# One block on one core: TensorE adds the rows of an expert pair before it runs the second tile's stage of that pair, and VectorE and ScalarE take its results one pair later

## What is computed

```
q = (ht @ w_q).reshape(T, PEER_HEADS, 2, PEER_HALF)
sc = jnp.einsum('thpc,hpnc->thpn', q, sub_keys)
s1, i1 = lax.top_k(sc[:, :, 0], 16);  s2, i2 = lax.top_k(sc[:, :, 1], 16)
top_s, pos = lax.top_k(s1[..., :, None] + s2[..., None, :], 16)   # flattened
eid = take_along_axis(i1 * 128 + i2, pos);  g = softmax(top_s)
a = einsum('cd,chkd->chk', hc, u_tab[ec])
y = einsum('chk,chkd->cd', gc * gelu(a), v_tab[ec])
x = x + gate2 * y
```

## Time and profile before

| | |
|---|---|
| median of three runs | 1017.3 us (1014.5 to 1018.57) |
| the profiled execution | 1019.0 us, span of its instructions 1017.2 us |
| busy: TensorE matmul / VectorE / ScalarE / GpSimd | 841.0 / 649.5 / 362.3 / 288.1 us |
| DMA | 351.95 MB, mean 346 GB/s |
| gathers of expert rows | 268.45 MB |

### The profile page before, as it was taken

The page is one execution under the profiler, slowest core; times in us unless marked ns, Lnnn a source line. Parts: engine busy times, 40 slices in busy tenths (PEclk is TensorE's granted clock), DMA queues, the critical chain, the costliest instruction groups (busy, mean ns, idle before and its releaser), DMA issues.

```text
span 1017.2 us, 9145 instructions
## 1 busy us (share of the span) xinstructions
PE 841.0 (83%) x2764; PEld 470.4 (46%) x2764; DVE 649.5 (64%) x1612; ACT 362.3 (36%) x1015; POOL 288.1 (28%) x275
## 2 busy tenths in 40 slices
PE   4889889998978888878987975988698777777776
PEld 4767656657943333333434533653263332222222
DVE  4799957723868587777543643975778644455444
ACT  2456434532235545654221231341233222222221
POOL 3000000000223334424422531335245343333330
PEclk9999979998998899979998987999899899999999
DMA  9958845547779699978999997999989999999995
GB/s 318 384 204 311 313 168 191 207 152 265 273 309 421 253 373 377 420 283 342 419 411 400 400 410 265 379 418 409 422 338 423 392 423 422 422 420 422 421 422 238
DMA packets 84872, 351.95 MB, mean 346 GB/s; under 512 B 6668, under 2 KB 19028, under 8 KB 52056
## 3 DMA queue, kind: packets, MB, share of 16 engines
q0 software_dynamic: 36864, 268.45, 65.2%
q1 hardware_dynamic: 46264, 82.89, 23.1%
q10 hardware_dynamic: 1696, 0.04, 0.1%
HBM read 350.31 MB, written 1.05 MB: 345 GB/s over the span
## 4 chain that ended last, share of the span: by engine, by line
PE 43%; DMA 27%; DVE 21%; issue 4%; ACT 3%; POOL 1%; ACTq 1%; SPq 1%; POOLq 0%; DVEq 0%
PE ps_y L1415 18%; DMA ring<-in_peer_uv,eid 15%; DVE ring L869 6%; DMA late_ring<-in_w_peer_q 4%; DMA out_y<-wide 3%; DMA late_ring<-in_w_out 3%; PE bank L1355 3%; PE bank L1364 2%; DMA late_ring<-in_w_up_moba 2%; PE bank L1380 2%; PE ps_y L1226 2%; PE bank L1226 2%; PE ps_y L1227 2%; PE ps_y L1228 2%; PE bank L1227 2%
## 5 line engine op out<-in xcount | busy, mean ns | idle before, releaser
L1415 PE MATMUL ps_y<-ring,diag 128*128 128x512 f32 x1024 | 491.4, 629 | 114.2 <-ACT diag L1130 112.9
L493 POOL DMA_INDIRECT ring<-in_peer_uv,eid x256 | 278.5, 1088 | 690.0 <-PE ps_y L1415 416.8
L869 DVE CUSTOM_DVE_ANT_0 ring<-ring,gates 128x1024 f32<-128x1024 f32 x256 | 307.7, 1224 | 183.8 <-DMA ring<-in_peer_uv,eid 182.7
L1415 PEld LDWEIGHTS ps_y<-ring,diag 128*128 128x128 f32 x1024 | 197.2, 200 | 382.9 <-issue 211.5
L1119 ACT ACTIVATE gel<-adot 128x2 f32<-128x2 f32 x128 | 26.0, 203 | 394.3 <-DVE adot L869 394.1
L1130 ACT ACTIVATE diag<-ident,ew 128x128 f32<-128x128 f32 x256 | 86.7, 386 | 0.0
L1123 ACT ACTIVATE ew<-g_sb,gel 128x1 f32<-128x1 f32 x256 | 61.5, 287 | 4.2
L956 ACT ACTIVATE w_hi<-ring 128x512 fp32r<-128x512 f32 x80 | 47.9, 626 | 29.5 <-PE bank L1228 28.1
L554 DVE TENSOR_TENSOR w_lo<-ring,w_hi 128x512 fp32r<-128x512 f32 x80 | 54.4, 690 | 4.4 <-PE ps_y L1228 1.9
L1226 PE MATMUL bank<-w_hi,hT_hi 128*128 128x512 f32 x96 | 40.4, 421 | 7.0 <-DVE w_lo L554 4.0
L1380 PE MATMUL bank<-tT,late_ring 128*128 128x128 f32 x256 | 31.6, 284 | 12.7 <-DMA late_ring<-in_w_peer_q 12.7
(11 more groups left out here) (184 smaller groups left out, 859.8 us busy)
## 6 DMA issues: line engine op xcount, KB each, us to landing
ring<-in_w_ada SPq DMA_DIRECT2D x12, 2048.0 KB, 9.0
ring<-in_w_in SPq DMA_DIRECT2D x10, 2048.0 KB, 8.0
ring<-in_w_peer_q SPq DMA_DIRECT2D x4, 2048.0 KB, 8.1
late_ring<-in_w_peer_q SPq DMA_DIRECT2D x8, 1024.0 KB, 21.8
ring<-in_w_out SPq DMA_DIRECT2D x2, 2048.0 KB, 10.8
ring<-in_peer_uv,eid POOLq DMA_INDIRECT x256
late_ring<-in_w_out SPq DMA_DIRECT2D x4, 1024.0 KB, 17.5
ring<-in_w_up_fox SPq DMA_DIRECT2D x1, 2048.0 KB, 9.1
```

Of the source, the lines that this page charges most:

```text
L493: pool.indirect_dma_start(uv_row(n), None, peer_uv, bass.IndirectOffsetOnAxis(ap=eid[:, n:n + 1], axis=0)).then_inc(s_uv[n % NP], 16)
L869: dve.tensor_tensor_reduce(u_row(n), u_row(n), h2[:, n // P, :], 1.0, 0.0, ALU.mult, ALU.add, adot[:, at:at + 1]).then_inc(s_dot, 1)
L1415: ins = pe.matmul(ps_y[:, cut], diag[:, n % ND, :], v_row(n)[:, cut], start=first, stop=last)
```

## The change

TensorE's loop now calls `add_rows(pair)` first and the stages of that slot after it. VectorE's and ScalarE's stages that take TensorE's results are laid one slot later, so that each is as far behind TensorE's as it was. `norm2`, tile 1's first choices (heads 0 and 1) and the first `choose_keys` of the loop move one slot later too. The other choices keep their slots: tile 0's at 4, 6, 13, 15, 17, 24, 26, 28, tile 1's at 59 to 82. So does `finish(0)` at 64. No instruction is added or removed.

```
-    "up": (35, 36, 39, 40), "up_dve": (36, 37, 40, 41),
+    "up": (35, 36, 39, 40), "up_dve": (37, 38, 41, 42),
     "mix": (40, 42),
-    "out": (43, 44, 47, 48), "out_dve": (44, 45, 48, 49),
-    "norm2": 50, "h2T": 51,
+    "out": (43, 44, 47, 48), "out_dve": (45, 46, 49, 50),
+    "norm2": 51, "h2T": 51,
     "queries1": (52, 53, 56, 57, 62, 63, 74, 75),
-    "keys": ((None, None, 2, 13, 24), (54, 59, 69, 78)),
-    "pairs": ((None, None, 4, 15, 26), (55, 61, 71, 80)),
-    "experts": ((None, None, 6, 17, 28), (56, 62, 73, 82)),
+    "keys": ((None, None, 3, 13, 24), (55, 59, 69, 78)),
+    "pairs": ((None, None, 4, 15, 26), (56, 61, 71, 80)),
+    "experts": ((None, None, 6, 17, 28), (57, 62, 73, 82)),
...
-def lay_attention(behind, attention):
+def lay_attention(behind, attention, later=0):
     for n, slot in enumerate(SLOT["attention"]):
-        lay(behind, slot, lambda n=n: attention(1, n // STEPS, range(n % STEPS, n % STEPS + 1)))
+        lay(behind, slot + later, lambda n=n: attention(1, n // STEPS, range(n % STEPS, n % STEPS + 1)))
...
-            lay_attention(behind, attention)
+            lay_attention(behind, attention, 1)
...
-                lay(behind, SLOT["queries0"][m - Q_FIRST], lambda m=m: queries(0, m))
-            lay_attention(behind, attention)
+                lay(behind, SLOT["queries0"][m - Q_FIRST] + 1, lambda m=m: queries(0, m))
+            lay_attention(behind, attention, 1)
             for h in range(2):
-                lay(behind, SLOT["mix"][h], lambda h=h: to_tT(1, "mixT", h))
-                lay(behind, SLOT["h2T"], lambda h=h: to_tT(1, "h2T", h))
+                lay(behind, SLOT["mix"][h] + 1, lambda h=h: to_tT(1, "mixT", h))
+                lay(behind, SLOT["h2T"] + 1, lambda h=h: to_tT(1, "h2T", h))
             lay(behind, SLOT["norm2"], norm2_root)
             for m in range(8):
-                lay(behind, SLOT["queries1"][m], lambda m=m: queries(1, m))
+                lay(behind, SLOT["queries1"][m] + 1, lambda m=m: queries(1, m))
...
             for pair in range(NG * PAIRS):
-                for stage in behind.get(pair, ()):
-                    stage()
                 if pair == HEADS * PAIRS:
                     pe.wait_ge(s_ytaken, 2)
                 add_rows(pair)
+                for stage in behind.get(pair, ()):
+                    stage()
```

## The result

| | median | lowest to highest | ratio to before, 95% interval |
|---|---|---|---|
| before, same chip | 1015.9 us (4 runs) | 1008.1 to 1018.6 | |
| changed kernel | 1035.1 us (4 runs) | 1031.2 to 1040.6 | 1.0206 [1.0132, 1.0280] |
| changed kernel, timed again | 1037.1 us (6 runs) | 1032.8 to 1037.7 | 1.0214 [1.0184, 1.0243] |

The changed kernel is 2.1% slower, 19 to 22 us by the medians. The forecast was 14 us, 1031.3, in a range of 1019 to 1041.

What follows compares the result with a forecast made beforehand. Gathers were taken to fill the DMA for most of the second half, so cost was priced as DMA idle time. Start 8.5, tile 0's choices 2, store 1.5, pairs 74 and 75 2: 1017.3 + 14 = 1031.3 us, range 1019 to 1041.

Steps and rivals of the forecast that it cites:

- The start: First pairs: tile 0's last queries run after adds, row 6 is issued later, first adds slow; 8.5 us, from 6 to 10.
- row 22: Tile 0's early gathers: row 22, issued at 338.65 before, comes some 7.4 us later, near 346.
- three waits: VectorE at score tiles: step 16's 5.70 us falls to some 2; steps 11 and 18 each get about 5.
- Tile 0's choices: Choices keeping their slots: net 6 us more waiting on VectorE, more than half hidden; 2 us, from -6 to +6.
- Pairs 63 to 75: Tile 1's later queries, late load and store: 1.5 us idle DMA for the store, 2 us at pairs 74 and 75.
- pair 63: Query moved from before pair 63's adds to before pair 64's, about 3 us later; costed at nothing, 3 if uncovered.
- pairs 74 and 75: Query now after pair 74's adds, adds of 76 to 78 3.7 us later; 2 us idle DMA, 0 to 4.
- The store term: VectorE at slot 71 waits 6 to 12 us for tile 0's stores, before 3.93; 1.5 us idle DMA, 0 to 5.
- (a): Rival, whole kernel: only the start costs, the moved choices cancel; 1021 to 1025 us, chance 0.16.
- (b): Rival, slot 26: separating step 16 from choose_pairs closes idle time, if row 6 comes before 297; 1013 us, chance 0.07.
- (c): Rival: slot 71 store wait uncovered (8), slot 59 keys stall 3, tile 0's waits in full (6); 1047 us, chance 0.09.
- (d): Rival, whole kernel: gathers fill the DMA whatever TensorE's order, so no change; 1017 us, chance 0.06.

Runs made afterwards that it cites:

- e12: Changed kernel with the start repaired, query blocks 4 to 7 of tile 1 one slot earlier; 1019.3 us, ratio 1.0034.
- e1: Kernel before with only the last two query blocks of tile 0 one pair later; 1023.4 us, ratio 1.0069.
- e3: Changed kernel with all later choices of VectorE one slot later too, start left late; 1023.2 us, ratio 1.0070.
- e4: Changed kernel with tile 0's last two query blocks back at the start and all choices one slot later; 1014.6 us, ratio 0.9991.
- e2: Changed kernel with the last two query blocks of tile 0 back ahead of the adds of pairs 0 and 1; 1023.1 us, ratio 1.0086.
- e6: Changed kernel with the start repaired and only tile 0's choices one slot later; 1020.2 us, ratio 1.0041.
- e7: Changed kernel with the start repaired and only tile 1's choices one slot later; 1021.9 us, ratio 1.0066.
- e8: Kernel before with the last two query blocks of tile 0 both ahead of the pair loop; 1017.6 us, ratio 1.0027.
- e10: Kernel before, but where a choice and an attention step share a slot, VectorE and ScalarE do the choice first; 1009.0 us, ratio 0.9939.
- e11: Changed kernel with the choice done before the attention step wherever they share a slot; 1023.2 us, ratio 1.0060.

## Why the prediction was right, and where its sizes were off

**The start: right, to the size.** Row 6 was to be 8.5 us later; it is 8.5 (30.4 against 21.9 us). Of that 1.4 us are the slow first adds (5.13 in place of 3.70 us, after 5.16 us of idling), taken at 1.2; the full price as in the earlier trace rows was 1.7. That the price could be read off the length of the gap was partly luck: at pair 63 a gap of 2.83 us was followed by adds of 5.40 us, at pair 74 of e12 one of 2.93 by adds of 3.70. In the time the start is 7.0 us (e1) to 8.0 (e3 less e4). The forecast row 22 "some 7.4 us later" was too short: it came 81.9 us after the first gather against 69.9, 12 us later. The hand working kept the old waits of slots 5 and 6 and so missed the 5.34 us at attention step 2 (2.04 before), of which 3.80 stand in e2 without a late row 6. I named three waits for tile 0's choices, and this is a fourth. I also priced start and choices as terms that simply add; some 2 us by pair 10 come only when both are there, and up to 5 in the time.

**Tile 0's choices: mechanism right, term too small.** The three waits were named with their places and came out as said (2.26, 5.91 and 5.52 us for "some 2" and "about 5"). The step that failed is the next one, "of which the rows in flight hide more than half: 2 us". Tile 0's choices cost 4.5 us (e2 less e6) to 7.6 (e7 less e4), 4 to 5 by the table at pair 34, against the 2 of the sum; next to the net 6 us of waits that the forecast had worked out, at most a third was hidden. Why so little was hidden is my reading: in this stretch the DMA isn't full (shares of 0.67 and 0.75 in the windows above), as the earlier trace rows had already shown for 333 to 341 and 427 to 465.

**Pairs 63 to 75: half right.** The two places were named, pair 63 at nothing ("if that cover is gone it is 3") and pairs 74 and 75 at 2 us. The queries put back (e12) give 5.2 us in the time, and by the table some 2 of them at pair 63 and the rest at pair 74. So the place priced at nothing isn't free. The store term, 1.5 us from a longer wait at slot 71, did not come. There the changed kernel has

```profile
735.51 0.19 DVE L791 CAST wide<-i 128x64 f32<-128x64 uint32 x1
```

without any wait, where the earlier trace rows had 3.93 us. That wait isn't a fixed property of the old slots either: in e1 and e8, which keep every slot of tile 1, it is gone as well, and in e10 it is 3.44 us. My reading of the changed kernel is that the adds of pair 64 came late, gathers were short for a while, and the DMA gave its time to the late loads and the store. The window and the issue row fit that (against the earlier trace rows), and so does VectorE at pair 68, which waits for a row instead:

```profile
700.00:717.00 17.00, 16.97 (x69) 9.88 (x68) 9.59 (x17) 4.63 (x17) 7.52 (x7) 0.98 1.03 372
```

```profile
late_ring<-in_w_peer_q SPq DMA_DIRECT2D x8, 1024.0 KB, 9.2
```

```profile
716.96 1.23 DVE L869 CUSTOM_DVE_ANT_0 ring<-ring,gates 128x1024 f32<-128x1024 f32 x1 [6.21 <-DMA ring<-in_peer_uv,eid]
```

I had taken the 21.8 us of a late load as a duration. It is no constant: the same median is 9.2 us in the changed kernel, 11.5 in e2, 17.8 in e1 and 25.2 in e10, the kernel whose gathers run ahead of all others. With a share of 1.03 the DMA was never idle in the window. The packet-by-packet turns of the Trainium skill ("DMA: Bandwidth & Descriptors", "Queues, rings and completion order") are consistent with either speed; an equal share by bytes was my reading of them, not a measurement.

**The rivals.** (a) "start only" is what e3 is, 7.1 us. (b) "faster" had a right place, step 16 with `choose_pairs` in slot 26; e10 wins some 4 us between pairs 10 and 34, but by turning the two round, not by moving the step, and the condition of (b), a row 6 ahead of 297, wasn't met (counted from the first gather). (c) had the waits of tile 0's choices in full, which came nearer than the forecast's 2 us, and a store term that didn't come; its 3 us at the keys of slot 59 are 0.74 in the changed kernel. (d) falls with all of them.

**Net.** Forecast 8.5 + 2 + 1.5 + 2 = 14. Measured against e4, which is 0.9 us below before: 8.0 for the start, 9.6 for all choices that stayed (with the queries behind them), 5.0 more with both, 21.7 in all by the second timing. The start had its size. The choices were allowed 4 us and cost 9.6, and the extra cost of both together wasn't in the sum; the 1.5 us for the store stood in for some of that by luck. The measured times lie in the range because the range was wide.

## What to carry to other kernels

Price a reordering by what stays in place: stages that all move together cost nothing measurable (e4), and the loss sits where a moved stage meets one with a fixed slot or a queue with a condition on it. Where an engine has both a result to await and work of its own in the same turn, try the own work first; here that alone was worth 0.6% (e10), and 1.5% where waits had piled up (e11). Don't credit rows in flight as cover for a wait without a row that shows it: here they hid little of tile 0's waits, and at pairs 63 and 74, where the DMA was nearly full before, they did not hide TensorE's lateness either.
